# A branch merge whose first weights are loaded and split one stage earlier, and two reordered passes on TensorE

## What is computed

```python
u = rmsnorm(h, mix_pre);  p = u @ w_in
o_rwkv, shift_new, wkv_new = rwkv_branch(p_rwkv, ...)      # shift_new = p[:, -1], rows of the projection
o_mla = mla_attention(...) @ mla_w_o
o_mem = mem_attend(q_mem, mem_k, mem_v) @ mem_w_o
g = sigmoid(gate_logits).reshape(B, T, 3, D)               # gate_logits = u @ w_in[:, gate columns]
merged = g[:, :, 0] * o_rwkv + g[:, :, 1] * o_mla + g[:, :, 2] * o_mem
h = h + rmsnorm(merged @ w_out, mix_post)
y = swiglu_half(h, ffn2_pre, ffn2_post, ffn2_gate, ffn2_up, ffn2_down)
```

## Time and profile before

| what | us |
|---|---|
| three timed runs | 3344.12, 3347.96, 3355.12 |
| their median | 3347.96 |
| the profiled execution, its own time | 3342.83 |
| its span in the trace | 3341.2 |
| mean granted TensorE clock | 0.974 of full speed |

### The profile page before, as it was taken

One profiled execution on the slowest core, in us unless ns is written; L12 is line 12 of the kernel. 1 busy time (PEld: TensorE's weight loads), 2 busy tenths in 40 slices (PEclk: granted clock), 3 DMA queues, 4 the chain that ended last, 5 costly groups with the idle time before them and its releaser, 6 DMA issues. The chain is left out here.

```text
span 3341.2 us, 61784 instructions
## 1 busy us (share of the span) xinstructions
PE 3173.2 (95%) x25520; PEld 2947.9 (88%) x25520; DVE 1636.4 (49%) x2881; ACT 926.3 (28%) x1681; POOL 297.3 (9%) x330
## 2 busy tenths in 40 slices
PE   7999999999999999968899989999998999999997
PEld 7999999998899989937777568888798999999997
DVE  4554455446545546556554533222226554445445
ACT  5212221214112222244654341212145211111112
POOL 0000000004001122240003000000014000000003
PEclk8999999999999999988999999999999999999998
DMA  6111111103422120002015641111033111111112
GB/s 193 38 39 62 38 50 38 50 30 111 131 84 68 52 83 4 17 7 58 15 43 175 220 143 48 40 45 47 26 102 114 51 38 50 50 50 38 43 37 85
DMA packets 257443, 218.30 MB, mean 65 GB/s; under 512 B 41682, under 2 KB 235004, under 8 KB 256629
## 3 DMA queue, kind: packets, MB, share of 16 engines
q1 hardware_dynamic: 252404, 196.33, 19.1%
q0 software_dynamic: 3824, 19.47, 1.7%
q10 hardware_dynamic: 1040, 0.00, 0.0%
HBM read 179.81 MB, written 35.96 MB: 65 GB/s over the span
## 5 line engine op out<-in xcount | busy, mean ns | idle before, releaser
L1458 PE MATMUL banks<-XR,wR 128*128 128x344 f32 x6336 | 1005.9, 320 | 7.3 <-DVE rs L1572 5.7
L1458 PEld LDWEIGHTS banks<-XR,wR 128*128 128x128 f32 x6336 | 1000.0, 189 | 7.9 <-issue 4.6
L1458 PE MATMUL banks<-hidR,wR 128*128 128x344 f32 x3168 | 511.0, 321 | 2.9 <-DVE tiles L1692 2.9
L1458 PEld LDWEIGHTS banks<-hidR,wR 128*128 128x128 f32 x3168 | 500.5, 188 | 9.2 <-DVE tiles L1692 4.6
L1069 PE MATMUL banks<-XR,pR 128*128 128x344 f32 (+1 forms) x1944 | 319.2, 325 | 3.6 <-DVE pR L2178 2.9
L1592 DVE TENSOR_TENSOR tiles<-tiles,banks 128x344 f32<-128x344 f32 x480 | 240.7, 512 | 165.8 <-PE banks L1458 165.0
L1069 PEld LDWEIGHTS banks<-XR,pR 128*128 128x128 f32 (+1 forms) x1944 | 312.6, 191 | 10.3 <-issue 6.1
L1069 PE MATMUL banks<-XR,gateR 128*128 128x344 f32 x1728 | 306.0, 333 | 14.6 <-DVE gateR L2956 7.8
L1541 ACT ACTIVATE sq<-sq 128x344 f32<-128x344 f32 x120 | 59.2, 493 | 926.5 <-DVE sq L1570 926.5
L1069 PEld LDWEIGHTS banks<-XR,gateR 128*128 128x128 f32 x1728 | 280.5, 191 | 29.8 <-issue 8.2
L1570 DVE TENSOR_TENSOR sq<-banks,shared 128x344 f32<-128x344 f32 x120 | 62.0, 516 | 365.9 <-PE banks L1458 365.8
(11 more groups left out here) (456 smaller groups left out, 3659.7 us busy)
## 6 DMA issues: line engine op xcount, KB each, us to landing
wraw<-in_ffn_down SPq DMA_DIRECT2D x22, 1024.0 KB, 4.9
wraw<-in_ffn_gate SPq DMA_DIRECT2D x43, 512.0 KB, 3.8
wraw<-in_ffn_up SPq DMA_DIRECT2D x43, 512.0 KB, 4.8
praw<-in_w_in SPq DMA_DIRECT2D x26, 512.0 KB, 4.3
tiles<-h_spill SPq DMA_DIRECT2D x9, 1376.0 KB, 6.8
tiles<-in_cache_mla SPq DMA_DIRECT2D x64, 144.0 KB, 3.1
tiles<-in_cache_mla POOLq DMA_DIRECT2D x64, 144.0 KB, 3.3
h_spill<-tiles SPq DMA_DIRECT2D x6, 1376.0 KB, 7.6
```

What stands on the lines that cost most here:

```text
L1458: ins = self.k.nc.tensor.matmul(out, wgt[:, a, cols], x(b)[:, grp(g)], start=first and n == 0, stop=last and n == 2)
```

## The change

1. The 14 transposes of the shift rows move behind the second group of the last tile, into a function `turn_rows` of their own.
2. The gate and output weights of branch 0 for pass 0 are loaded in the memory attention, after "o1", into `sq` and `w_o`; ACT takes the high part after step 12 (L4432 of the changed kernel), DVE the low part at its end (L4546). `tail` starts with these there: SP only counts their semaphores up, and PE, ACT and DVE have no first wait. For this the rooms of branches 0 and 2 are exchanged (`HOME`, `raw`), since the third part of `gateR` is free by then.
3. The last pass goes through the branches as (0, 1, 2). What hangs on places in that order (`split`, `lows`, first loads and splits of `w_out`) moves to the same places of the new order.

```diff
@@ -2147,6 +2147,8 @@
         k, nc, n, vec = self.k, self.k.nc, self.n, self.vec
         for i in range(2, self.N):
             for g in range(NT):
+                if i == self.N - 1 and g == NT - 1:
+                    self.turn_rows(pe)
                 self.product(pe, i, g)
             if 3 <= i < 7:
                 vec.sums(pe, i - 3)
@@ -2156,14 +2158,16 @@
                 vec.spread(pe, i - 12)
             if 17 <= i < 21:
                 vec.decay(pe, i - 17)
-            if i == self.of["p", 11]:
-                self.mixed.wait(pe, i)
-                vec.act_s.wait(pe, ("s", RT - 1))
-                for q in range(4):
-                    for j in range(4 * q, min(4 * q + 4, n)):
-                        ins = nc.tensor.transpose(k.ps[q][0:DEC + 1, (j % 4) * P:(j % 4 + 1) * P], self.last_p[:, j, :],
-                                                  k.ident[:, :])
-                    ins.then_inc(self.rows_ready.sem, 1)
+
+    def turn_rows(self, pe):
+        k, nc, n = self.k, self.k.nc, self.n
+        self.mixed.wait(pe, self.of["p", 11])
+        self.vec.act_s.wait(pe, ("s", RT - 1))
+        for q in range(4):
+            for j in range(4 * q, min(4 * q + 4, n)):
+                ins = nc.tensor.transpose(k.ps[q][0:DEC + 1, (j % 4) * P:(j % 4 + 1) * P], self.last_p[:, j, :],
+                                          k.ident[:, :])
+            ins.then_inc(self.rows_ready.sem, 1)
 
     def high(self, act, i):
         act.wait_ge(self.landed[i % 2].sem, 16 * (i // 2 + 1))
...
+    HOME = (2, 1, 0)
...
-        self.raw = [k.C[:, 20, 0:D], k.C[:, 21, 0:D], k.sq[:, 1, 0:D]]
-        self.parts = [k.gateR[:, b] for b in B3]
+        self.raw = [k.sq[:, 1, 0:D], k.C[:, 21, 0:D], k.C[:, 20, 0:D]]
+        self.parts = [k.gateR[:, self.HOME[b]] for b in B3]
...
-        self.by = (1, 2, 0)
+        self.by = (0, 1, 2)
         self.last = [(b, g) for g in range(NT) for b in self.by]
-        self.last_work = [("w", 1), (1, 0), ("w", 2)] + self.last[1:]
+        self.last_work = [("w", 1), self.last[0], ("w", 2)] + self.last[1:]
...
-        for b in self.B3:
+        sp.sem_inc(self.gate_landed[0].sem, 16)
+        sp.sem_inc(self.out_landed[0].sem, 16)
+        for b in (1, 2):
             self.load_gate(sp, b, 0)
             self.load_out(sp, b, 0)
-        sp.wait_ge(self.first_split.sem, 1)
         self.load_gate(sp, 0, 1)
...
     def on_pe(self, pe):
         NB = self.NB
         self.pe_s.prime(pe)
-        pe.wait_ge(self.first_split.sem, 1)
         with pe.Fori(0, DT - 1) as j:
...
-        act.wait_ge(self.gate_landed[0].sem, 16)
-        nc.scalar.activation(self.parts[0][:, 0, :], self.raw[0], ACT.Copy).then_inc(self.first.sem, 1)
...
-        split = {(1, 1): (0, 0), (2, 1): (0, 1), (1, 2): (1, 0), (2, 2): (1, 1)}
+        split = {(0, 1): (0, 0), (1, 1): (0, 1), (0, 2): (1, 0), (1, 2): (1, 1)}
...
-        dve.wait_ge(self.first.sem, 1)
-        nc.vector.tensor_tensor(self.parts[0][:, 1, :], self.raw[0], self.parts[0][:, 0, :].bitcast(F32), ALU.subtract)\
-            .then_inc(self.first_split.sem, 1)
...
-        lows = {(2, 1): 0, (2, 2): 1}
+        lows = {(1, 1): 0, (1, 2): 1}
...
-        self.raw = [k.C[:, 20, 0:D], k.C[:, 21, 0:D]]
+        self.raw = [k.C[:, 21, 0:D], k.C[:, 20, 0:D]]
...
+        pairs = [[blocks(merge.parts[b][:, a]) for a in range(2)] for b in range(2)]
+        halves = [[merge.parts[b][:, a] for a in range(2)] for b in range(2)]
...
     def first_loads(self, sp):
         self.merge.dve_l.wait(sp, ("w", 1))
-        self.merge.dve_s.wait(sp, ("w", 0), DT - 2)
         self.load(sp, 0)
+        self.merge.dve_l.wait(sp, ("w", 2))
         self.load(sp, 1)
...
     def first_high(self, act, i):
-        self.merge.pe_l.wait(act, (1 + i, NT - 1))
+        self.merge.pe_l.wait(act, (i, NT - 1))
...
+    gate_landed, gate_high = Count(k, "mem_gate_weights_landed"), Count(k, "mem_gate_weights_high")
+    gate_raw, gate_parts = k.sq[:, 1, 0:D], k.gateR[:, Merge.HOME[0]]
...
             sp.dma_start(k.mem_raw, k.mem_q[:, :, 0:SEQ]).then_inc(landed_all_q.sem, 16)
             for i in range(4, 2 * DEC):
                 fetch(i)
+            pe_s.wait(sp, "o1")
+            sp.dma_start(gate_raw.rearrange("p (f c) -> p f c", f=DT), k.io["w_in"][0].rearrange("(f p) n -> p f n", p=P)
+                         [:, :, COL_GATE:COL_GATE + P]).then_inc(gate_landed.sem, 16)
+            sp.dma_start(k.w_o[:, 0, :].rearrange("p (f c) -> p f c", f=4),
+                         k.io["rwkv_w_o"][0].rearrange("(f p) n -> p f n", p=P)[:, :, 0:P]).then_inc(gate_landed.sem, 16)
+            sp.wait_ge(gate_landed.sem, 32)
 
         @block.gpsimd
         def _(pool):
...
                 pe_s.wait(act, ("o", n))
                 h, j = divmod(n, NQ // 2)
                 act_s.done(nc.scalar.activation(out[:, h, 2 * j * P:(2 * j + 2) * P], k.ps[5][:, 0:2 * P], ACT.Copy), ("o", n))
+                if n == 12:
+                    act.wait_ge(gate_landed.sem, 32)
+                    nc.scalar.activation(gate_parts[:, 0, :], gate_raw, ACT.Copy).then_inc(gate_high.sem, 1)
 
         @block.vector
         def _(dve):
...
+            dve.wait_ge(gate_high.sem, 1)
+            nc.vector.tensor_tensor(gate_parts[:, 1, :], gate_raw, gate_parts[:, 0, :].bitcast(F32), ALU.subtract)
```

More of the change, by code:

```diff
@@ L2801, in __init__ @@
                                                    [("gate",) + m, ("mult",) + m, m])])
-        self.first = Count(k, "merge_first_weights_high")
-        self.first_split = Count(k, "merge_first_weights_split")
         self.gate_w = k.io["w_in"][0].rearrange("(f p) n -> p f n", p=P)
@@ L3326, in _ @@
         def _(act):
-            m.on_act(act, {(1, 2): lambda act: mix.first_high(act, 0), (2, 2): lambda act: mix.first_high(act, 1)})
+            m.on_act(act, {(0, 2): lambda act: mix.first_high(act, 0), (1, 2): lambda act: mix.first_high(act, 1)})
             m.high(act, NT - 1, range(DT))
@@ L3366, in _ @@
         def _(dve):
-            m.on_dve(dve, {(1, 2): lambda dve: mix.low(dve, 0), (2, 2): lambda dve: mix.low(dve, 1)})
+            m.on_dve(dve, {(0, 2): lambda dve: mix.low(dve, 0), (1, 2): lambda dve: mix.low(dve, 1)})
             m.low(dve, NT - 1)
```

8 lines of the change are left out of this document (3 added, 5 removed).

## The result

The changed kernel took 3328.1 us (median of four runs, 3324.09 to 3332.17) against 3350.1 us for the kernel before (the three known runs and a fourth of 3352.26): 22.0 us less, a ratio of 0.994 with an interval of 0.9926 to 0.9954, which is 15.4 to 24.8 us. On three other chips the difference of the medians was 22.8, 22.5 and 24.0 us. The forecast was 3323 in a range of 3313 to 3334, from a sum of 22.6.

What follows compares the result with a forecast made beforehand. PE was taken as the bound, busy 95% of the span, losing time to four waits and slow matmuls behind them. Gains 5.6 + 7.1 + 9.9 = 22.6 us off 3346.0 gave 3323 us, range 3313 to 3334.

Steps and rivals of the forecast that it cites:

- Part 1: Shift rows' transposes: the 3.36 us wait goes and the clock stays up; gain 5.6 us, between 3.36 and 5.9.
- best bound: Shift rows: the upper end of the gain, 5.9 us, with transposes at 0.12 us each.
- row of four memory-attention loads: Memory attention: four loads in 0.57 us, about 0.14 each, used to price the 14 transposes at 2.0 us.
- Part 2: Merge's start: first product 5.07 us earlier and 2.02 shorter at full clock; gain 7.1 us, 5.1 if the clock falls.
- terms for the barrier and the entry: Merge's start: SP's first instruction behind the barrier at 1979.23, then 0.46 us for PE to enter its loop.
- Rival A: Merge's start: the clock falls all the same after 1.7 us of pause; 2.0 us less gain, 3325; chance 0.17.
- The loads: Memory attention: 768 KB land by 1966.8 even behind all of u_low, ACT asks at 1969.1; no wait.
- Part 3: Last pass: nine products in 54.7 us, not 64.62, no wait left; gain 9.9 us, 6.8 if only waits go.
- covers of 2.2 and 2.4 us: Last pass: weights of branches 1 and 2 are split 2.2 and 2.4 us before PE asks for them.
- B: Waits go but slow stretches come by themselves at other places: gain 15.3 us, 3331; chance 0.08.
- C: Merge's start: something else holds PE as long and the copy's 1.06 stays: gain 14.4 us, 3332; chance 0.06.
- D: Memory attention: slower, ACT stands at the new copy until both loads land; a landing at 2002 gives 3356; chance 0.03.

Runs made afterwards that it cites:

- first pair: The first profiled executions of the kernel before (3342.83 us) and of the changed kernel (3332.17 us).
- the kernel with part 1 alone: Kernel before with only the shift rows' transposes moved ahead of the last product: 3341.7 us against 3347.3, ratio 0.9982.
- the kernel with part 3 alone: Kernel before with only the branch rooms exchanged and the last pass in order 0, 1, 2: 3335.7 us, 11.6 less, ratio 0.9969.
- first and third series: Two chips; the changed kernel beside it without its early merge weights: 3324.6 against 3331.2 us in the first, 3323.5 against 3328.9 in the third.
- first profile: The changed kernel's first profiled execution, 3332.17 us, the longest of its four.
- second series: One chip: changed kernel, 3325.5 us; with copy moved and unread products added, 3323.3; copy at step 10, 3325.8; loads exchanged, 3327.3.

## Why the prediction came out right

The time fell inside the range, on the side and near the size forecast: 3328.1 against 3323. Of the miss, 4.1 us are the base: the fourth run of the kernel before lifted its median to 3350.1, where 3346.0 was taken. The difference itself was 22.0 where the sum said 22.6. That they lie so near is in part luck, as the interval of 15.4 to 24.8 us says; what bears the account is the traces.

**Part 1**, forecast 5.6: 5.94 in the first pair, 5.98 in the kernel with part 1 alone, 5.6 timed. Against the 23.49 us that the old order took in the kernel with part 3 alone it would be 5.1. The wait went, the clock stayed at 1.00, the transposes ran without a pause. The one term clearly off was their price: 14 in 1.45 us, 0.10 each, below the 2.0 taken and below the 1.7 of the best bound; the way to the scan, carried over whole, took 0.1 more (5.66 us against 5.54). The row of four memory-attention loads was not near enough; why they take longer there isn't shown. What hangs behind was as foreseen: ScalarE's copies ended at 1175.6 by the rows above, SyncE's stores follow, the last eviction waits for TensorE alone.

**Part 2**, forecast 7.1 with the clock up and 5.1 with it down: 7.1 where it stayed up (first and third series), 5.8 where it fell (first profile). The copy cost 0.95 for 1.06, within its bounds. The terms for the barrier and the entry were 0.2 short together: the first gate product came 1.46 us after the last result copy's end (1.45 when the clock fell), 1.24 was the sum's. **Rival A** had the price of 2.0 and the chance of 0.17. Its event came in the first profile and cost 1.2 by the forecast's measure (7.28 - 6.08; 1.36 against the 5.92 of the profiles where the clock stayed up), not 2.0, since the slow stretch ended within the first product. The clock fell in the window from 1983, less than 2 us after TensorE's last work at 1982.04: that so short a pause keeps the clock up, as the forecast took it, didn't hold in this one. In seven profiles of kernels that start the merge like this it came once; in all six of kernels with the old start and its wait of 7.7 to 8.2 us the clock was at half there. So 0.17 was a fair chance for an event that one execution has and the next one hasn't, and the step to correct is its form: the same kernel, the changed one, had it in one of four profiles.

The Trainium skill, "TensorE: Matmul & The Clock Gate", Part 4: PE-mode transpose, says that transposes don't count as TensorE's activity in the way of matmuls. No run here shows that it does or doesn't bear on this start: what TensorE runs ahead of it is the same in the profile with the fall and in the six without, and the one kernel with products added had nothing to prevent.

**The loads**: no wait, as forecast, but not by the working of the forecast. The 768 KB were not carried behind `u_low` at its rate: the first load passed ahead of it in 3.9 us, the second landed with it, 15.6 us after its issue, at 1969.8 with the ask at 1973.2. Set against the copy's place this is a cover of 3.4 us; the forecast had 2.3, so its sum was on the safe side by a picture that the trace doesn't bear out. The experiment with the copy at step 10 shows the edge.

**Part 3**, forecast 9.9: 9.85 in the trace of the changed kernel and of the one with part 3 alone, 54.77 us for nine products where 54.7 was worked out. Both covers of 2.2 and 2.4 us held. Timed, the part alone gave 11.6, with 9.9 inside its interval of 6.7 to 13.7.

**Rivals B, C and D** did not come: no slow stretch stands at the two other places, TensorE starts the merge 1.87 us after its last work, and ScalarE waits for no DMA. What B said of the clock was true in another way: slow stretches do come in one execution and not in the next, in code that the change doesn't touch. Over the fourteen profiles the head up to the eviction of `p` 11 took 1157.9 to 1165.8 us and the stretch from the scan to the memory attention 747.2 to 752.0. By these two alone (7.9 and 4.8 us) two single spans could lie up to 12.7 us apart, more than half of what the change gains; the range had 10 for its base and the best bounds together.

## What to carry to other kernels

Price a wait of TensorE at its length plus the slow matmuls behind it, but carry the second term as a range: the same wait of 3.45 us was followed by none in two profiles and by 1.4 us in a third. Measure each part between marks at its own place, in several profiles, before subtracting spans; a difference of 2 to 4 us that seemed to belong to the change in ten profiles wasn't there on the next chip. Put the kernels with and without the change on the same chip before you group them. And work that is moved into a neighbouring stage is free only in a real gap: the same copy cost 0.95 us behind a result and nothing ahead of that result, in ScalarE's idle time.

## What the runs showed of the hardware

A load of 256 KB issued 0.1 us before a 4 MB load of another queue landed with it or up to 1.6 us later, after 15.4 to 15.7 us in eight profiles; one of 512 KB issued 0.4 us before the small one was done in 3.9 to 4.2. With the two exchanged it was 15.3 for the 512 KB and 2.9 for the 256 KB. I had reckoned both behind the large one. At which gap between the issues it turns, no run tells.

Unchanged code took up to 8 us more or less in one execution than in another. From the scan's first product to the memory attention the traces show two things that differ. One is TensorE's clock 255 us into the scan, here in the kernel with the loads exchanged (windows):

```profile
1434.00:1437.00 3.00, 3.00 (x6) 1.39 (x6) 2.97 (x8) 1.48 (x4) 2.38 (x3) 0.54 0.27 44
```

From ScalarE's copy ahead of it (L929) to the load of its function table behind it (L919) this kernel took 1441.49 - 1433.54 = 7.95 us. The changed kernel of the third series, with a clock of 1.00 there, took 1437.50 - 1430.59 = 6.91. So the stretch costs about 1.0 us, and it stands in four of the fourteen profiles.

The other is time in which TensorE waited for nothing that the profile shows ("issue"), in the midst of its groups of small products. Both lines are of the changed kernel, in the first 260 us of the scan (waited for: us in total, times, longest), first in the second series, then in the third:

```profile
PE banks L385 <- issue: 6.1, 15, 1.0
```

```profile
PE banks L385 <- issue: 3.4, 9, 1.0
```

That is 2.7 of the 3.4 us by which these two executions of one kernel differ in the stretch (751.0 against 747.6). Over all profiles it is 4.6 to 6.1 us in the six long ones and 3.4 to 5.0 in the eight short ones, so the two groups overlap. What TensorE waits for there, and why all four kernels of the second series had the long form, stays open.
